# Keys projected in halves inside the recurrence of a two-block fp32 network

## The chip, the cores and the metric

One core of a Trainium2 chip runs the whole program in one launch. The metric is the time of one execution on the device in microseconds (us), lower is better; three runs of the kernel before gave 3436.60, 3443.00 and 3440.77.

## The reference

The input is 512 tokens of width 1024, all fp32. First come two mixing layers of three branches, with a feed-forward part behind each, then a second block that the change does not touch (a pooling layer and a dilated attention layer). A mixing layer, cut to what matters here:

```python
z = rms(x) @ w_in                            # conv q/k, v, o, gates, s_q, ckv, i_q, i_k, d_q, d_k, d_v, ...
h = mlstm(mq, mk, mv, i_pre, f_pre)          # recurrence over 4 chunks of 128 tokens, 4 heads of 128
y_a = sigmoid(m_o) * rms(h)
kv  = rms(s_ckv) @ w_kv_up                   # sparse keys and values
sq, sk = rope(rms(s_q)), rope(rms(kv[0]))    # 8 heads of 64; index scores choose 128 keys per token
y_b = sparse_attention(sq, sk, kv[1], rope(i_q), rope(i_k), i_w)
dq, dk = rope(rms(d_q)), rope(rms(d_k))      # 8 half heads of 64
y_c = rms(diff_attention(dq, dk, d_v, lam))
x = x + merged(gates, y_a, y_b, y_c) @ w_out
```

## The kernel before, in words

**Weights.** Every weight matrix comes as chunks of up to 128 x 1024 fp32. SP loads each into one of four slots RAW (`load`, line 316 on). POOL splits each into a high part WH and a low part WL with two slots each (`split`, L374, L375, L378), and may start on a chunk as soon as TensorE has finished the chunk two before it (`chunk_done`). TensorE multiplies high by high, high by low and low by high: `by_columns` (L405) with weights stationary, `by_tokens` (L454) with tokens stationary, two k tiles, four token tiles and 512 columns a chunk, so 24 matmuls.

**Order.** There is no planner. Each engine has a program written out by hand, and semaphores named after events tie them together; `claim(bank)` makes TensorE wait until the last reader of a PSUM bank has signalled. In a mixing layer TensorE does: convolution inputs, the small gates, ckvq, sq, mv, mo (lines 504 to 538); the sums of the gates (L542, L543, bank 5, copied by VectorE in L1554); transposes of the compressed keys and sparse queries (`to_features`, L492); kvup, two chunks that give sparse keys and values (L555, L558); the transposes of index queries and keys; then the recurrence.

**Recurrence** (lines 571 to 627 on TensorE, 1561 to 1639 on VectorE, 1159 to 1171 on ScalarE). For each of four chunks of tokens: a diagonal (L1565) is spread over the partitions by a ones matmul (L576), VectorE takes maxima and writes the arguments (L1569 to L1586), ScalarE takes exponentials, VectorE multiplies with q k (L581) in L1592 and weights the values (L1597); TensorE forms the state products (L596), turns the product (L604), forms the carried part (L613) and the values (L623); VectorE adds (L1606, L1614), updates the state (L1622 to L1627), divides and writes HALL (L1635 to L1638).

**After it.** TensorE projects the queries (dq), turns HALL and the sparse keys, projects the keys (dk), forms the index scores (L649), projects the values (dv) and turns queries and keys (lines 629 to 663). VectorE norms h, then runs `norm_and_turn` (line 1467: reductions of squares L1430, reciprocal L1423, tables L1451 to L1453, and for each of four tiles L1471, L1461, L1462, L1464, L1465) for the sparse keys, the queries and, after the index masks (lines 1657 to 1673), the keys. ScalarE, all of whose activations have line 1030, copies banks out, takes squares and roots. Then come the attentions, whose scores are L717 and which are interleaved with the gates (L679, L687).

Of the kernel before, what the change touches and what calls it, by code (L numbers as in the profile page):

```python
# [13 lines left out]
P = 128  # L14
T = 512
# [96 lines left out]
ROOTS = {"ckv": (256, 4), "sq": (S_DH, 32), "h": (M_DH, 16), "sk": (S_DH, 32), "dq": (S_DH, 32),  # L112
# [4 lines left out]
def build(nc, dram, weights, out):  # L117

    ctx = ExitStack()
    with ctx:  # L120
# [54 lines left out]
        SQUARED = {"ckv": TB[:, :, 0:256], "sq": TA, "h": HALL, "sk": TA, "dq": TB, "dk": TA}  # L175

        def square_of(name, m, width):
            where = YC[:, m, :] if name in ("ckv", "sq", "h") else MS[:, m * T:(m + 1) * T]
            return where[:, 0:width]
# [21 lines left out]
        RTOK = tiny(4)  # L201

# [183 lines left out]
        def _(pe):  # L386
# [53 lines left out]
            def by_tokens(outs, c, slot, ks, cols, hi, lo, n_k, shared=False):  # L440


                turns = [(w, n) for w in (WH, WL) for n in range(NT)]
# [52 lines left out]
            def layer(li):  # L496
# [37 lines left out]
                for name, banks, sem in (("ckvq", (5, 6, 7, 0), "ckvq_raw"), ("sq", (1, 2, 3, 4), "sq_raw"),  # L534
                                         ("mv", (5, 6, 7, 0), "v_ready"), ("mo", (1, 2, 3, 4), "mo_ready")):
# [23 lines left out]
                for n, b in enumerate((0, 1, 2, 3)):  # L559
# [6 lines left out]
                            lambda f: L("tr_copied", 9))  # L566


                pe.wait_ge(*L("mqk_ready", 8))
                pe.wait_ge(*L("v_ready", NT))  # L570
                for n in range(NT):
# [13 lines left out]
                    if n < NT - 1:  # L585
# [6 lines left out]
                        claim(2, 3)  # L592
# [8 lines left out]
                    claim(4)  # L601
                    pe.wait_ge(*L("sw_ready", n + 1))
                    for h in range(M_HEADS):
                        mm = nc.tensor.transpose(PS[4][:, h * P:(h + 1) * P], DM[:, h * P:(h + 1) * P],  # L604
                                                 IDENT[:, :])
                    mm.then_inc(L("swt_ready"), 1)
                    release[4] = L("swt_copied", n + 1)
# [1373 lines left out]
def lay_out(inputs):  # L1981
# [53 lines left out]
    def col(v):  # L2035
        return v.reshape(-1, P).T
# [57 lines left out]
```

## Time and profile before

| what | value |
| --- | --- |
| median of three runs | 3440.77 us |
| the profiled execution | 3439.93 us |
| its span, first to last instruction | 3438.3 us |
| mean granted TensorE clock | 0.954 |
| layer 0: projections end, recurrence starts, last totals, first scores | 168.85, 193.50, 259.10, 371.20 us |
| layer 1: the same | 1255.8, 1281.4, 1344.7, 1456.7 us |
| busy POOL | 1844.4 us, 54% |

The granted clock is 1.00 at 2.4 GHz and 0.50 at 1.2 GHz. Busy time of one instruction includes what it is held up in its engine. Matmuls follow each other faster than their durations say, since they overlap.

### The profile page before, as it was taken

What the parts mean: (1) busy time and instruction counts of PE and PEld (TensorE: products, weight loads), DVE (VectorE), ACT (ScalarE), POOL (GpSimd) and SP (SyncE); (2) the same over time, 40 slices, a digit from 0 to 9 for tenths busy, and PEclk for the clock granted to TensorE, in tenths of its full rate; (3) what the DMA queues carried; (4) which work ended last, traced back from release to release, by engine and by line L of the source; (5) the groups of instructions that cost most, each with busy time, mean ns of one, the idle gap of its engine ahead of it and who ended that gap; (6) DMA issues with size and microseconds to landing.
All of it is one profiled execution on the core that took longest, in us unless ns stands there. A gap on an engine that the chain in (4) does not pass through costs nothing.

```text
span 3438.3 us, 39007 instructions
## 1 busy us (share of the span) xinstructions
PE 3125.3 (91%) x14414; PEld 2575.1 (75%) x14414; DVE 1676.1 (49%) x2578; ACT 563.7 (16%) x1112; POOL 1844.4 (54%) x1621
## 2 busy tenths in 40 slices
PE   7957879999999986788999999989999999998998
PEld 5746657778878775666778887777778888887876
DVE  7647773464433665786265442455432222223543
ACT  2222223110000222223311000100011111121000
POOL 5603434566667651333366666675565555443665
PEclk9978989999999997898999999999999999999999
DMA  4201112233323320111133333332322222222322
GB/s 134 86 19 47 56 37 62 95 92 98 98 83 105 114 80 25 40 56 46 53 115 95 94 98 88 98 86 79 92 90 75 74 80 74 70 66 60 98 88 77
DMA packets 85371, 268.29 MB, mean 78 GB/s; under 512 B 9856, under 2 KB 10496, under 8 KB 85248
## 3 DMA queue, kind: packets, MB, share of 16 engines
q1 hardware_dynamic: 85248, 266.64, 25.7%
q8 instruction: 78, 1.28, 0.2%
q14 instruction: 45, 0.37, 0.0%
HBM read 262.41 MB, written 4.19 MB: 78 GB/s over the span
## 4 chain that ended last, share of the span: by engine, by line
PE 78%; DVE 17%; ACT 3%; issue 2%; DMA 0%; SPq 0%; DVEq 0%; POOL 0%; ACTq 0%
PE PS L405 52%; PE PS L454 11%; PE PS L687 3%; PE PS L679 3%; DVE MSK L1685 2%; DVE SMALLS L1684 2%; PE PS L915 1%; PE PS L740 1%; PE PS L941 1%; DVE MS L1730 1%; DVE TA L1471 1%; ACT MS L1030 1%; DVE TA L1465 1%; DVE SQ L1464 1%; PE PS L728 1%
## 5 line engine op out<-in xcount | busy, mean ns | idle before, releaser
L378 POOL TENSOR_TENSOR WL<-RAW,WH 128x1024 fp32r<-128x1024 f32 (+3 forms) x538 | 1208.2, 2246 | 44.8
L374 POOL TENSOR_TENSOR POOL_C<-POOL_C 128x1 f32<-128x1 f32 x538 | 124.2, 231 | 1525.7 <-PE PS L405 775.2
L405 PE MATMUL PS<-XNH,WH 128*128 128x512 f32 x1752 | 694.2, 396 | 14.8 <-DVE EYL L1401 9.1
L405 PE MATMUL PS<-XNL,WH 128*128 128x512 f32 x1752 | 686.5, 392 | 0.0
L375 POOL TENSOR_SCALAR WH<-RAW 128x1024 fp32r<-128x1024 f32 (+3 forms) x538 | 533.9, 992 | 0.3 <-issue 0.2
L405 PE MATMUL PS<-XNH,WL 128*128 128x512 f32 x1752 | 432.9, 389 | 0.0
L405 PEld LDWEIGHTS PS<-XNH,WH 128*128 128x128 f32 x1752 | 330.8, 189 | 88.3 <-DVE EYL L1401 10.3
L405 PEld LDWEIGHTS PS<-XNL,WH 128*128 128x128 f32 x1752 | 330.9, 189 | 69.1 <-issue 1.0
L405 PEld LDWEIGHTS PS<-XNH,WL 128*128 128x128 f32 x1752 | 328.2, 187 | 69.0
L454 PE MATMUL PS<-WH,XNH 128*128 128x512 f32 (+1 forms) x768 | 288.7, 376 | 0.0
L454 PE MATMUL PS<-WH,XNL 128*128 128x512 f32 (+1 forms) x768 | 286.9, 374 | 0.0
L1924 DVE SCALAR_TENSOR_TENSOR OQK<-PS,RT 128x512 f32<-128x512 f32 x48 | 33.1, 692 | 312.9 <-PE PS L405 307.0
L454 PE MATMUL PS<-WL,XNH 128*128 128x512 f32 (+1 forms) x768 | 176.0, 371 | 0.0
L454 PEld LDWEIGHTS PS<-WH,XNH 128*128 128x128 f32 x768 | 145.8, 190 | 22.6 <-issue 1.5
L454 PEld LDWEIGHTS PS<-WH,XNL 128*128 128x128 f32 x768 | 145.7, 190 | 20.3
L679 PE MATMUL PS<-XNH,WH 128*128 128x512 f32 x384 | 158.2, 412 | 0.0
L454 PEld LDWEIGHTS PS<-WL,XNH 128*128 128x128 f32 x768 | 140.9, 188 | 20.0
L679 PE MATMUL PS<-XNL,WH 128*128 128x512 f32 x384 | 152.4, 397 | 0.0
L405 PE MATMUL PS<-HH,WH 128*128 128x512 f32 x352 | 139.4, 396 | 7.3 <-DVE HL L1401 7.3
L405 PE MATMUL PS<-HL,WH 128*128 128x512 f32 x352 | 139.1, 395 | 0.0
L1799 DVE TENSOR_TENSOR HT<-SILU,PS 128x512 f32<-128x512 f32 x44 | 30.3, 688 | 202.1 <-PE PS L405 199.6
L1401 DVE TENSOR_TENSOR HL<-HT,HH 128x512 f32 (+1 forms) x44 | 112.6, 2559 | 5.1
(341 smaller groups left out, 4753.0 us busy)
## 6 DMA issues: line engine op xcount, KB each, us to landing
RAW<-w_oslot SPq DMA_DIRECT2D x56, 512.0 KB, 3.6
RAW<-w_L0ffn SPq DMA_DIRECT2D x44, 512.0 KB, 3.6
RAW<-w_L1ffn SPq DMA_DIRECT2D x44, 512.0 KB, 3.6
RAW<-w_od SPq DMA_DIRECT2D x32, 512.0 KB, 3.6
RAW<-w_epool SPq DMA_DIRECT2D x24, 512.0 KB, 3.6
RAW<-w_oslot SPq DMA_DIRECT2D x32, 384.0 KB, 3.0
RAW<-w_eug SPq DMA_DIRECT2D x16, 512.0 KB, 3.7
RAW<-w_eout SPq DMA_DIRECT2D x16, 512.0 KB, 3.6
```

The costliest lines, as they stand in the source:

```text
L374: nc.gpsimd.tensor_tensor(POOL_C[:, 1:2], POOL_C[:, 0:1], POOL_C[:, 0:1], ALU.add)
L375: nc.gpsimd.tensor_scalar(WH[:, half, 0:w], RAW[:, slot, 0:w], 1.0, 0.0, ALU.mult, ALU.add).then_inc(S("high_ready"), 1)
L378: nc.gpsimd.tensor_tensor(WL[:, half, 0:w], RAW[:, slot, 0:w], WH[:, half, 0:w].bitcast(F32), ALU.subtract).then_inc(S("weights_split"), 1)
L405: mm = nc.tensor.matmul(bank, w[:, slot, k * cols:(k + 1) * cols], x[:, k0 + k, :], start=first and j == 0 and w is WH and x is hi, stop=l ...
L454: mm = nc.tensor.matmul(outs[n], x[:, k, n * P:(n + 1) * P], w[:, slot, j * cols:(j + 1) * cols], start=k == 0 and w is WH and x is hi, st ...
L679: nc.tensor.matmul(PS[b][:, :], WH[:, c % 2, k * P:(k + 1) * P], x[:, k, :], start=k == 0 and x is XNH, stop=False)
L687: mm = nc.tensor.matmul(PS[b][:, :], WL[:, c % 2, k * P:(k + 1) * P], XNH[:, k, :], start=False, stop=k == KD - 1)
L728: mm = nc.tensor.transpose(PS[4][:, m * P:(m + 1) * P], SS[:, q % 2, src, m * P:(m + 1) * P], IDENT[:, :])
L740: mm = nc.tensor.matmul(PS[7][:, h * d:(h + 1) * d], TB[:, j, m * P:(m + 1) * P], V[:, m, h * d:(h + 1) * d], start=m == 0, stop=m == n)
L1401: V.tensor_tensor(dst_lo, src, dst_hi.bitcast(F32), ALU.subtract).then_inc(sem, 1)
L1684: then(V.max(TOP8, m))
L1685: then(V.match_replace(m, TOP8, m, TAKEN))
```

## The change

The query projection dq is placed behind mo, in banks 5, 6, 7, 0, and its raw values go to YA (as DQR). The key projection becomes two segments, dkA and dkB, of four chunks each with the same weights: each chunk is loaded and split twice, and TensorE multiplies it with token tiles 0 and 1 in the first segment and 2 and 3 in the second, 12 matmuls a time, one chunk behind the key transposes and one behind the values of each chunk of the recurrence (`half_of_keys`), in banks 4 and 5. The raw keys go to TB (as DKR). VectorE takes the roots of queries and sparse keys ahead of the recurrence and keeps them (RSQ, RSK, both new), keeps two sets of tables, and norms and turns one of eight tiles at each of eight places in the recurrence (`fill`). Inside the recurrence the state products move behind the carried part, the last chunk's are skipped as before, and the banks are dealt out anew. Behind it come the transposes of queries, dv, HALL, the index scores, sparse keys and keys; VectorE norms the keys ahead of the low halves and the masks. Four chunks a layer are added.

The diff, cut. What is left out: `by_tokens` gets a parameter `tiles`; the order of ROOTS, the buffers of squares (HALL for dq and sk) and the arguments `keep` and `t`; `norm_tile` is the body of the loop of `norm_and_turn`; the weights of dkA and dkB on the host.

```diff
--- before
+++ after
@@ -55,8 +55,8 @@
-    ("mv", 4, [1024]), ("mo", 4, [1024]), ("kvup", 2, [1024]),
-    ("dq", 4, [1024]), ("dk", 4, [1024]), ("dv", 4, [1024]),
+    ("mv", 4, [1024]), ("mo", 4, [1024]), ("dq", 4, [1024]), ("kvup", 2, [1024]),
+    ("dkA", 4, [1024]), ("dkB", 4, [1024]), ("dv", 4, [1024]),
     ("gA", 8, [1024, 512]), ("gC", 8, [1024, 512]), ("gB", 8, [1024, 512]), ("wout", 8, [1024]),
...
@@ -532,7 +534,8 @@
-                                         ("mv", (5, 6, 7, 0), "v_ready"), ("mo", (1, 2, 3, 4), "mo_ready")):
+                                         ("mv", (5, 6, 7, 0), "v_ready"), ("mo", (1, 2, 3, 4), "mo_ready"),
+                                         ("dq", (5, 6, 7, 0), "dq_raw")):
...
@@ -564,7 +567,21 @@
+                pe.wait_ge(*L("tr_copied", 9))
+                def half_of_keys(step):
+                    name, q = ("dkA", "dkB")[step // 4], step % 4
+                    tiles = (0, 1) if name == "dkA" else (2, 3)
+                    if q == 0:
+                        claim(4, 5)
+                    c = seg(name) + q
+                    by_tokens({n: PS[4 + n % 2][:, :] for n in tiles}, c, c % 2, (2 * q, 2 * q + 1), T,
+                              XNH, XNL, KD, tiles=tiles)
+                    if q == 3:
+                        for n in tiles:
+                            release[4 + n % 2] = L("dk_raw", n + 1)
...
@@ -589,6 +606,25 @@
+                    half_of_keys(2 * n)
+                    claim(b)
+                    pe.wait_ge(*L("sw_ready", n + 1))
+                    for h in range(M_HEADS):
+                        mm = nc.tensor.transpose(PS[b][:, h * P:(h + 1) * P], DM[:, h * P:(h + 1) * P],
+                                                 IDENT[:, :])
...
+                        for h in range(M_HEADS):
+                            mm = nc.tensor.matmul(
+                                PS[(1, 7 - n % 2)[h // 2]][:, h % 2 * 129:h % 2 * 129 + 129],
+                                MQK[:, h, tok], CT[:, h * 129:(h + 1) * 129], start=True, stop=True)
+                        mm.then_inc(L("n2_ready"), 1)
+                        release[1] = release[7 - n % 2] = L("n2_taken", n)
+                    if n < NT - 1:
                         claim(2, 3)
                         pe.wait_ge(*L("ktm_copied", n + 1))
                         pe.wait_ge(*L("vw_ready", n + 1))
...
@@ -598,66 +634,41 @@
                     mm.then_inc(L("n1_ready"), 1)
-                    release[banks[0]] = release[banks[1]] = L("tot_ready", n + 1)
-                token_group(f"L{li}dq", (1, 2, 3, 4))
-                for n, b in enumerate((1, 2, 3, 4)):
-                    release[b] = L("dq_raw", n + 1)
+                    release[1] = release[0] = L("tot_ready", n + 1)
+                    half_of_keys(2 * n + 1)
+                pe.wait_ge(*L("dq_normed", 1))
+                to_features(lambda n, f: DQR[:, n, f * P:(f + 1) * P], 4, (6, 7, 2, 3), L("tr_ready"),
+                            lambda f: L("tr_copied", f + 10))
+                token_group(f"L{li}dv", (0, 1, 4, 5))
+                for n, b in enumerate((0, 1, 4, 5)):
+                    release[b] = L("dv_ready", n + 1)
                 pe.wait_ge(*L("ya_tm", NT))
-                to_features(lambda n, f: HALL[:, n, f * P:(f + 1) * P], 4, (0, 5, 6, 7), L("tr_ready"),
+                to_features(lambda n, f: HALL[:, n, f * P:(f + 1) * P], 4, (6, 7, 2, 3), L("tr_ready"),
                             lambda f: L("ya_low", f + 1))
-                pe.wait_ge(*L("sk_normed", 1))
-                to_features(lambda n, f: TA[:, n, f * P:(f + 1) * P], 4, (5, 6, 7, 0), L("tr_ready"),
-                            lambda f: L("tr_copied", f + 14))
-                token_group(f"L{li}dk", (1, 2, 3, 4))
-                for n, b in enumerate((1, 2, 3, 4)):
-                    release[b] = L("dk_raw", n + 1)
-                pe.wait_ge(*L("tr_copied", 9))
                 for n in range(1, NT):
...
                     for h in range(IDX_HEADS):
-                        b = (5, 6, 7, 0)[h]
+                        b = (0, 1, 4, 5)[h]
...
-                token_group(f"L{li}dv", (1, 2, 3, 4))
-                for n, b in enumerate((1, 2, 3, 4)):
-                    release[b] = L("dv_ready", n + 1)
-                pe.wait_ge(*L("dq_normed", 1))
-                to_features(lambda n, f: TB[:, n, f * P:(f + 1) * P], 4, (5, 6, 7, 0), L("tr_ready"),
+                pe.wait_ge(*L("sk_normed", 1))
+                to_features(lambda n, f: TA[:, n, f * P:(f + 1) * P], 4, (6, 7, 2, 3), L("tr_ready"),
                             lambda f: L("tr_copied", f + 18))
                 pe.wait_ge(*L("dk_normed", 1))
...
@@ -1141,50 +1152,57 @@
+                chunk(seg("dq") + 4)
+                for n, b in enumerate((5, 6, 7, 0)):
+                    run(DQR[:, n, :], PS[b][:, :], ACT.Copy, L("dq_raw"), scale=RTOK[:, n:n + 1])
                 for f in range(2):
                     take(6 + f, CKVH[:, f, :], T, f + 1)
                 for f in range(4):
                     take(f, SQT[:, f, :], T, f + 3)
+                root("dq")
                 if li:
                     act.wait_ge(S("x_saved"), 16 * KD)
                 chunk(seg("kvup") + 1)
                 for n, b in enumerate((4, 5, 6, 7)):
                     run(TA[:, n, :], PS[b][:, :], ACT.Copy, L("sk_raw"))
+                square("sk")
                 chunk(seg("kvup") + 2)
                 for n, b in enumerate((0, 1, 2, 3)):
                     run(SV[:, n, :], PS[b][:, :], ACT.Copy, L("sv_ready"))
                 for f in range(2):
                     take(4 + f, IQT[:, f, :], T, f + 7)
                 take(6, IKT[:, :], T, 9)
+                root("sk", squares=False)
...
+                    if n == 2:
+                        chunk(seg("dkA") + 4)
+                        for m in range(2):
+                            run(DKR[:, m, :], PS[4 + m][:, :], ACT.Copy, L("dk_raw"), scale=RTOK[:, m:m + 1])
                     act.wait_ge(*L("darg_ready", n + 1))
...
                         act.wait_ge(*L("n1_ready", n))
-                    run(SWT, PS[4][:, :], ACT.Copy, L("swt_copied"))
+                    run(SWT, PS[6 + n % 2][:, :], ACT.Copy, L("swt_copied"))
+                chunk(seg("dkB") + 4)
+                for m in range(2, 4):
+                    run(DKR[:, m, :], PS[2 + m][:, :], ACT.Copy, L("dk_raw"), scale=RTOK[:, m:m + 1])
                 root("h")
-                chunk(seg("dq") + 4)
-                for n, b in enumerate((1, 2, 3, 4)):
-                    run(TB[:, n, :], PS[b][:, :], ACT.Copy, L("dq_raw"), scale=RTOK[:, n:n + 1])
-                root("sk")
                 for f in range(4):
-                    take((0, 5, 6, 7)[f], YAH[:, f, :], T, f + 10, scale=col(li, "m_norm_g")[:, f:f + 1])
-                square("dq")
+                    take((6, 7, 2, 3)[f], DQT[:, f, :], T, f + 10)
+                root("dk")
+                chunk(seg("dv") + 4)
+                for n, b in enumerate((0, 1, 4, 5)):
+                    run(DV[:, n, :], PS[b][:, :], ACT.Copy, L("dv_ready"), scale=RTOK[:, n:n + 1])
                 for f in range(4):
-                    take((5, 6, 7, 0)[f], SKT[:, f, :], T, f + 14)
-                root("dq", squares=False)
-                chunk(seg("dk") + 4)
-                for n, b in enumerate((1, 2, 3, 4)):
-                    run(TA[:, n, :], PS[b][:, :], ACT.Copy, L("dk_raw"), scale=RTOK[:, n:n + 1])
-                square("dk")
-                act.wait_ge(*L("dq_normed", 1))
...
@@ -1550,6 +1570,8 @@
+                squares(S_HEADS, "dq", keep=RSQ)
+                dq_tables = rope_tables(row("dq_g"), 1)
...
@@ -1557,6 +1579,17 @@
+                dve.wait_ge(*L("tr_ready", 9))
+                sk_tables = rope_tables(row("sk_g"))
+                squares(S_HEADS, "sk", keep=RSK)
+                def fill(step):
+                    if step < 4:
+                        norm_tile(DQR, step, RSQ, dq_tables, "dq")
+                    else:
+                        norm_tile(TA, step - 4, RSK, sk_tables, "sk")
...
@@ -1587,6 +1620,7 @@
+                    fill(2 * n)
...
@@ -1607,8 +1641,9 @@
+                    fill(2 * n + 1)
                     dve.wait_ge(*L("n1_ready", n + 1))
-                    for e, b in enumerate((5, 0)):
...
@@ -1646,12 +1681,8 @@
-                dve.wait_ge(*L("sk_raw", NT))
-                dve.wait_ge(*L("tr_ready", 9))
-                norm_and_turn(TA, "sk_g", "sk")
-                low_halves((0, 5, 6, 7), YAH, YAL, 10, "ya_low", gain=lambda f: col(li, "m_norm_g")[:, f:f + 1])
-                dve.wait_ge(*L("dq_raw", NT))
-                norm_and_turn(TB, "dq_g", "dq")
+                norm_and_turn(DKR, "dk_g", "dk")
+                low_halves((6, 7, 2, 3), YAH, YAL, 14, "ya_low", gain=lambda f: col(li, "m_norm_g")[:, f:f + 1])
...
@@ -1671,8 +1702,6 @@
-                dve.wait_ge(*L("dk_raw", NT))
-                norm_and_turn(TA, "dk_g", "dk")
```

## Rows read from the trace of the kernel before

**Rows 1.** The page's part 1: busy time, share and instructions of each engine.
```profile
...
PE 3125.3 (91%) x14414; PEld 2575.1 (75%) x14414; DVE 1676.1 (49%) x2578; ACT 563.7 (16%) x1112; POOL 1844.4 (54%) x1621
```

**Rows 2.** Stages: stretch, length, busy PE, PEld, DVE, ACT, POOL; PEclk, DMA share, GB/s.
```profile
...
168.85:177.15 8.30, 3.20 (x29) 2.96 (x28) 7.91 (x27) 5.35 (x10) 3.62 (x3) 0.97 0.41 125
177.15:189.70 12.55, 12.54 (x50) 10.26 (x51) 0.71 (x2) 2.07 (x4) 3.59 (x3) 0.88 0.07 7
189.70:193.50 3.80, 1.31 (x12) 1.08 (x11) 0.00 (x0) 3.54 (x7) 3.55 (x3) 1.00 0.28 114
193.50:259.10 65.60, 36.65 (x150) 30.50 (x151) 32.88 (x96) 9.97 (x19) 0.00 (x0) 0.66 0.03 8
259.10:371.20 112.10, 84.09 (x378) 68.72 (x376) 88.57 (x122) 31.82 (x59) 47.54 (x36) 0.85 0.17 50
1255.80:1264.10 8.30, 3.22 (x29) 2.96 (x29) 7.92 (x26) 5.35 (x10) 3.60 (x3) 0.88 0.37 123
1264.10:1277.60 13.50, 13.48 (x50) 10.89 (x51) 0.72 (x2) 2.07 (x5) 3.59 (x3) 0.82 0.06 11
...
1281.40:1344.70 63.30, 34.84 (x149) 29.05 (x150) 32.87 (x96) 9.97 (x19) 0.00 (x0) 0.68 0.03 9
```

**Rows 3.** The chain that ended last, layer 0: start, us, engine and line.
```profile
...
259.00 21.80 PE PS L454 x96
```

**Rows 4.** PE's timeline, layer 0: start, us, line, tiles, idle time and its releaser.
```profile
...
177.16 0.77 PE L454 MATMUL PS<-WH,CKVH 128*128 128x512 f32 x1 [5.11 <-DVE SMALLS L1554]
```

**Rows 5.** Stretches on DVE: stretch, length, busy (operations), PEclk, DMA share, GB/s.
```profile
...
135.20:158.20 23.00, 22.58 (x21) 1.00 0.33 92
288.00:299.40 11.40, 10.99 (x21) 0.50 0.00 0
...
264.20:275.90 11.70, 11.43 (x9) 1.00 0.20 52
332.30:341.20 8.90, 7.71 (x15) 0.73 0.09 28
```

**Rows 6.** Timeline around 138 us, POOL and DVE.
```profile
...
138.29 2.71 POOL L378 TENSOR_TENSOR WL<-RAW,WH 128x1024 fp32r<-128x1024 f32 x1
...
138.78 2.77 DVE L1471 TENSOR_TENSOR TA<-TA,SMALLS 128x512 f32<-128x512 f32 x1
```

**Rows 7.** Timeline of one chunk (n = 1) of the recurrence, layer 0.
```profile
...
210.94 2.05 PE L576 MATMUL PS<-MS,ONES 128*128 128x512 f32 x2 [3.42 <-DVE MS L1565]
...
215.98 0.69 DVE L1586 TENSOR_TENSOR MS<-MS,SMALLS 128x512 f32<-128x512 f32 x1
...
217.47 0.69 DVE L1592 TENSOR_TENSOR MS<-MS,PS 128x512 f32<-128x512 f32 x1 [0.80 <-ACT SMALLS L1030]
...
218.91 2.06 PE L596 MATMUL PS<-MS 128*128 128x129 f32 x8 [3.94 <-DVE MS L1597]
...
221.62 1.93 PE L613 MATMUL PS<-MS,MQK 128*128 128x129 f32 x8
...
223.34 1.61 PE L623 MATMUL PS<-VEXT,MS 128*128 128x129 f32 x8
...
225.05 0.76 DVE L1614 TENSOR_TENSOR MS<-MS,PS 128x258 f32<-128x258 f32 x2 [0.71 <-PE PS L623]
...
229.78 2.05 PE L576 MATMUL PS<-MS,ONES 128*128 128x512 f32 x2 [4.83 <-DVE MS L1565]
```

**Rows 8.** Groups of ACT, 259.1 to 300 us: count, busy us, mean ns, idle before.
```profile
...
L1030 ACT ACTIVATE MS<-TA 128x512 f32<-128x512 f32 x4 | 2.2, 642 | 0.0
...
L1030 ACT ACT_TABLE_LOAD x1 | 1.3, 1283 | 0.0
```

**Rows 9.** Groups of DVE, 281 to 288 us.
```profile
...
L1430 DVE TENSOR_REDUCE SMALLS<-MS 128x8 f32<-128x512 f32 x4 | 2.5, 678 | 8.1 <-ACT MS L1030 8.1
...
L1451 DVE TENSOR_TENSOR TMP<-COS,ROW 128x256 f32<-128x256 f32 x1 | 0.4, 426 | 0.0
L1423 DVE RECIPROCAL SMALLS<-SMALLS 128x32 f32<-128x32 f32 x1 | 0.4, 354 | 0.4 <-ACT SMALLS L1030 0.4
```

More of the change, by code:

```diff
@@ L173, in build @@
         SS = MS[:, :].rearrange("p (b j w) -> p b j w", b=2, j=4)
-        SQUARED = {"ckv": TB[:, :, 0:256], "sq": TA, "h": HALL, "sk": TA, "dq": TB, "dk": TA}
+        DQR, DKR = YA, TB
+        SQUARED = {"ckv": TB[:, :, 0:256], "sq": TA, "h": HALL, "sk": TA, "dq": DQR, "dk": DKR}
         def square_of(name, m, width):
-            where = YC[:, m, :] if name in ("ckv", "sq", "h") else MS[:, m * T:(m + 1) * T]
-            return where[:, 0:width]
+            where = {"ckv": YC, "sq": YC, "dq": HALL, "sk": HALL, "h": YC}.get(name)
+            return MS[:, m * T:m * T + width] if where is None else where[:, m, 0:width]
         at = [0]
@@ L438, in first_pair, with by_tokens @@
                     mm.then_inc(S("chunk_done"), 1)
-            def by_tokens(outs, c, slot, ks, cols, hi, lo, n_k, shared=False):
-                turns = [(w, n) for w in (WH, WL) for n in range(NT)]
+            def by_tokens(outs, c, slot, ks, cols, hi, lo, n_k, shared=False, tiles=range(NT)):
+                turns = [(w, n) for w in (WH, WL) for n in tiles]
                 if shared:
@@ L1194, in layer @@
                         w = (n + 1) * P
-                        run(RELU[:, i % 2, 0:w], PS[(5, 6, 7, 0)[h]][:, 0:w], ACT.Relu, L("relu_ready"))
-                root("dk", squares=False)
-                chunk(seg("dv") + 4)
-                for n, b in enumerate((1, 2, 3, 4)):
-                    run(DV[:, n, :], PS[b][:, :], ACT.Copy, L("dv_ready"), scale=RTOK[:, n:n + 1])
+                        run(RELU[:, i % 2, 0:w], PS[(0, 1, 4, 5)[h]][:, 0:w], ACT.Relu, L("relu_ready"))
                 for f in range(4):
-                    take((5, 6, 7, 0)[f], DQT[:, f, :], T, f + 18)
+                    take((6, 7, 2, 3)[f], SKT[:, f, :], T, f + 18)
                 for f in range(4):
-                    take((1, 2, 3, 4)[f], DKT[:, f, :], T, f + 22)
+                    take((0, 1, 4, 5)[f], DKT[:, f, :], T, f + 22)
                 for a in range(2):
@@ L1417, in over, with ask_root, squares @@
                     return ap.unsqueeze(1).to_broadcast([P, h, ap.shape[-1]])
-                def ask_root(name):
+                def ask_root(name, keep=None):
                     _, n = ROOTS[name]
                     dve.wait_ge(*L("root_taken", ROOT_NO[name]))
-                    then(V.reciprocal(RSH[:, 0:n], RSH[:, 0:n]))
-                def squares(h, name):
+                    then(V.reciprocal((RSH if keep is None else keep)[:, 0:n], RSH[:, 0:n]))
+                def squares(h, name, keep=None):
                     for n in range(NT):
@@ L1465, in turn, with norm_tile @@
                     return V.tensor_tensor(dst, straight, turned, ALU.add)
+                def norm_tile(buf, n, roots_, tables, name):
+                    then(V.tensor_tensor(heads(buf[:, n, :], 8), heads(buf[:, n, :], 8),
+                                         bcast(roots_[:, 8 * n:8 * n + 8], 8, S_DH), ALU.mult))
+                    ins = turn(buf[:, n, :], 8, tables[0][:, n, :], tables[1][:, n, :],
+                               heads(buf[:, n, :], 8))
+                    if n < NT - 1:
+                        then(ins)
+                    else:
+                        ins.then_inc(L(f"{name}_normed"), 1)
+                        dve.wait_ge(*L(f"{name}_normed", 1))
                 def norm_and_turn(buf, gain, name):
                     squares(S_HEADS, name)
[L1469 removed]
+                    tables = rope_tables(row(gain))
                     for n in range(NT):
[L1471 to L1477 removed]
+                        norm_tile(buf, n, RSH, tables, name)
                 then(V.memset(CONVIN[:, :, 0:3], 0.0))
```

54 lines of the change are left out of this document (20 added, 34 removed).

## The prediction

> **What bounds the kernel now.** The page comes first: TensorE is busy for 91% of the span [rows 1], so a gain has to come from time in which it waits or runs at its lower clock. The table of stages says where that is [rows 2]. I call P the end of the last projection (168.85 us in layer 0), S the start of the recurrent part (193.50), R the moment at which VectorE adds the last chunk's totals (259.10), and Q the first attention scores (371.20). From P to Q 202.3 us pass; layer 1 has the same legs, 25.6 us to S and 63.3 to R. In the recurrence TensorE is busy 36.6 of 65.6 us at a mean granted clock of 0.66, VectorE 32.9 us, POOL never. After it, TensorE is busy 84.1 of 112.1 us, VectorE 88.6.
>
> The chain of waits gives the reason for the tail: the query projection runs bare for 21.8 us [rows 3], then VectorE norms the sparse keys with TensorE idle, and the last thing before Q is VectorE's norm of the keys. Ahead of the recurrence TensorE stands 5.1 us until VectorE has copied the gate sums out of bank 5 (line 1554) [rows 4]. So this stretch is a relay: TensorE streams while VectorE has little, then VectorE turns tiles while TensorE has nothing. Two prices matter most [rows 5]: four tiles normed and turned take 11.4 us with POOL silent and 23.0 us with POOL splitting weights, 2.85 against 5.7 us a tile. Why shows in [rows 6]: a multiply of VectorE with both inputs in SBUF, 0.69 us elsewhere [rows 7], starts just after POOL's subtraction and ends only behind it, 2.77 us long.
>
> The Trainium skill ("SBUF — State Buffer", the section "Who interferes with whom") has the rule: a GpSimd operation and a VectorE one with two SBUF inputs exclude each other for a whole instruction. The trace agrees (0.69 against 2.77 us). It speaks against this change.
>
> **The change, part by part.** I add in three legs, each against the same leg of before.
>
> *Leg 1, P to S.* The query projection moves here: four chunks, 21.8 us [rows 3]. It covers the tile work of VectorE that ran past P, which should end TensorE's 5.1 us wait. But what is late next is the same bank 5: VectorE copies the gate sums only after the squares of the queries and their tables. I follow ScalarE from P+21.8: four copies of queries, two and four transposed tiles, ten activations in 5.35 us [rows 2], P+27.2; four squares, 2.2, P+29.4; one more table load, 1.3 [rows 8], P+30.7. The reductions run beside the squares; root and reciprocal 0.8, three table products 1.1, the copy 0.2 [rows 9], so kvup starts at P+33 instead of P+8.3. Its 48 matmuls take 12.55 us as before (13.5 in layer 1), since the idle time ahead of them (about 7 us) again lets the clock fall. From the end of kvup to S it was 3.8 us. Now VectorE must wait for the index-key transposes (1.3), make the sparse keys' tables while POOL splits the next chunk (until 3.6 us after kvup [rows 2]), reduce four squares (2.5 [rows 9]), take the reciprocal behind the root (0.8) and form the diagonal (0.7): 7.7. So P to S is 33 + 13 + 7.8 = 53.8 us against 24.7 and 25.6: **+28.7**, that is 21.8 for the projection and 7 of new waiting.
>
> The Trainium skill ("ScalarE: Activation LUTs", the section "What ACT_TABLE_LOAD costs") puts another 1.38 us of drain behind each load; by the page leg 1 would be 1.4 longer. No row shows it: the load of [rows 8] is 1.28 us and nothing follows it.
>
> *Leg 2, S to R.* I walk one middle chunk, PE's spread of the diagonal at 0 [rows 7]. The arguments are ready at 5.75, as before. Then a tile, 2.85, takes the place of the 0.80 us wait for the exponential: 8.6. Product 0.7: 9.3. TensorE has meanwhile run its half of a key chunk, 12 matmuls, from 4.0 to 6.7 at the higher clock or 9.4 at the lower (half of the 5.4 us of a whole chunk, or twice that half), so it is mostly hidden. Turning the product 0.9, carried part 1.7, VectorE's read 0.8: 12.7. The second tile: 15.5. TensorE needs until 15.6 for the state products (2.0, now behind the carried part) and the values (1.5). From the totals to the next spread it was 4.7: 20.3, against 18.8 before. The second half chunk lies beside those 4.7 us.
>
> On top comes POOL: eight chunks instead of none are split here, 3.6 us each [rows 2], and each starts when a half chunk ends. Its bounds: nothing, if it falls on reductions, on operations reading PSUM or on VectorE's waits, and 2.9 us where SBUF work wants to run (the 11.6 us between the two prices of [rows 5], over four splits). Laid beside the walk, the first split of a chunk delays the weighting of the values a little, the second the division, HALL and the diagonal by some 2 us. I take 1.7 a period: 22. The first chunk has no carried part but its first split falls on a tile: 20.8; the last ends at its totals, 15.5. Sum 20.8 + 22 + 22 + 15.5 = 80.3 against 65.6 and 63.3: **+15.8**. Bounds: 70 with no blocking and the higher clock, 103 with full blocking and the lower one.
>
> The four extra chunks a layer cost 512 KB each on a queue that is nearly idle here (DMA share 0.03 [rows 2]); SP issues them as slots come free and nothing else is queued there. Nothing, unless POOL's ring falls behind the halves; at one split in 10 us it does not.
>
> *Leg 3, R to Q.* The query chunks (21.8) and key chunks leave it, and so do two norms. VectorE now sets it. HALL is ready at about R+3. The key copies stand ahead of the squares of h on ScalarE, then squares, load, root: multiplies from R+6.5. They take 8.6, between 5.5 (eight by 0.69) clean and 11.7 with POOL at two splits [rows 5], as one split meets them here: R+15. Reductions, root, reciprocal and tables 4.4: R+19.5. Four tiles 11.4, plus 2.9 for each of two splits of dv: R+36.7. Low halves four by 0.7: R+39.4. Masks 8.9 [rows 5]: R+48.3. ScalarE's last two index copies done, it moves eight tiles at 0.54 [rows 2], then scores: R+53. dv itself (21.8) ends near R+27 and is hidden. Against 112.1: **-59.1**. Bounds: 48 and 60.
>
> Per layer 28.7 + 15.8 - 59.1 = -14.6, for two layers -29.2 us. The profiled execution is 3439.93, 0.8 below the median of 3440.77, so I set the sum against the median: **3411.6**. Moved banks, YA and TB as buffers, and the kept roots change no duration; POOL's 28 us more of splits have no other cover to lose.
>
> **The rivals.**
> (1) *POOL and VectorE lock each other through the recurrence: slower.* Place: leg 2. Each of eight splits costs its full 2.9 to 3.6 us instead of the 0.6 that I count on average, +19, and at the lower clock the half chunks (5.4 us each) push the spread of the diagonal back, +4. Leg 2 is then 103 us, the layer +8: 3457. It decides from a period of 26.5 us on, where the 14.6 are used up. For it: [rows 5] and [rows 6]. Against: at least 5 us of VectorE's period read PSUM or reduce, 4 are waits. The rule from the skill named above gives this result. Chance 0.12.
> (2) *The denser stream keeps the clock high.* Filled periods have TensorE busy some 16 of 20 us where it was 10 of 18.8, and the clock fell in those gaps. Spread, carried part and values would lose half their time, about 2 us a period, kvup 1.6: 10 a layer more: 3392. Against: VectorE is nearly closed up, so shorter matmuls only shorten its waits. Chance 0.20.
> (3) *The new waits are larger than walked.* The bank 5 wait and the root chain of h behind the key copies each cost 4 us more: 3428. Chance 0.22.
> (4) *Nothing to measure:* 3441. The freed tail is just given back by legs 1 and 2, leg 2 at 95 us. Chance 0.10.
> Forecast itself 0.36.
>
> **How the numbers follow.** About 0.2%, 7 us, is what a measurement can tell from no change. Forecast, (2) and most of (3) are faster by more: 0.73. (4) and a bit of (3): 0.13. (1) and the edge of (4): 0.14. The range runs from just under (2) to short of (4): 3388 to 3438; it leaves out (1) and most of (4), which hold 0.2.
>
> **What would show it.** Right: TensorE still stands about 7 us ahead of kvup, with the copy of the gate sums as releaser; S at P+54; periods of 21 to 23 us in the recurrence; POOL busy some 29 us there; dk_normed near R+37; scores at R+53; P to Q near 188 us in both layers. Wrong: kvup starting at P+27, periods above 26.5 or under 19, or a tail over 60 us.

## The result, and the profile after

Four runs of the changed kernel gave 3414.81 to 3420.44 us, median 3416.36, against 3439.92 for the kernel before beside it: a ratio of 0.9934 (0.9916 to 0.9951). The forecast was 3411.6. The profiled execution is 3414.81 us, its span 3412.6, 25.7 less than before.

The page's parts 1 and 2 of the kernel after:

```profile
span 3412.6 us, 39047 instructions
...
PE 3113.2 (91%) x14414; PEld 2558.3 (75%) x14414; DVE 1681.3 (49%) x2578; ACT 564.2 (17%) x1114; POOL 1867.9 (55%) x1645
...
PEclk9988889999999997888999999999999999999999
```

TensorE runs as many matmuls as in [rows 1] and is busy 12 us less; POOL has the 24 instructions of eight more splits, three each. Between S and R it runs 21 instructions, so seven splits: the first two of the eight key chunks are split ahead of S, and the first chunk of values is split ahead of R. The table of stages of the kernel after, first three stages for leg 1 (P is 167.13, the first stretch starts 0.17 us behind it), then legs 2 and 3, then legs 2 and 3 of layer 1; columns as in [rows 2]:

```profile
167.30:199.84 32.54, 25.48 (x126) 20.81 (x124) 14.63 (x34) 11.44 (x20) 18.05 (x15) 0.98 0.33 95
199.84:213.47 13.63, 13.63 (x50) 11.01 (x51) 0.00 (x1) 4.26 (x8) 3.59 (x3) 0.80 0.06 9
213.47:221.98 8.51, 1.31 (x13) 1.10 (x11) 6.49 (x9) 3.86 (x8) 3.81 (x3) 0.81 0.36 112
221.98:305.95 83.97, 54.01 (x235) 43.17 (x236) 66.21 (x137) 9.57 (x18) 27.69 (x21) 0.76 0.16 44
305.95:357.25 51.30, 41.18 (x196) 32.10 (x194) 42.43 (x66) 24.04 (x46) 18.87 (x15) 0.85 0.12 37
1290.90:1377.40 86.50, 54.17 (x235) 43.44 (x236) 68.20 (x137) 9.58 (x18) 27.37 (x21) 0.76 0.15 43
1377.40:1428.80 51.40, 41.37 (x195) 32.23 (x193) 42.42 (x66) 24.00 (x46) 18.88 (x15) 0.85 0.13 36
```

The legs, layer 0 / layer 1, in us (an ordinary table, worked out from such rows of each kernel):

| leg | before | after | change | forecast |
| --- | --- | --- | --- | --- |
| 1, P to S | 24.7 / 25.6 | 54.8 / 54.4 | +30.1 / +28.8 | +28.7 |
| 2, S to R | 65.6 / 63.4 | 84.0 / 86.5 | +18.4 / +23.1 | +15.8 |
| 3, R to Q | 112.1 / 111.8 | 51.3 / 51.5 | -60.8 / -60.3 | -59.1 |
| P to Q | 202.3 / 200.8 | 190.1 / 192.3 | -12.2 / -8.5 | -14.6 |

Legs 1 and 3 are within 1.7 us of the working. Leg 2 is 2.6 and 7.3 us over. The two layers together gain 20.7 us where 29.2 were forecast; the span is 25.7 shorter, so 5 us more come from code that the change does not touch. Nearly all of it lies between Q of layer 0 and P of layer 1: 884.7 us before, 879.3 after, and 878.6 to 887.5 in the ten kernels below, which have the same code there. I can't tell these 5 us from such variation.

What stands ahead of the first product of kvup, PE's timeline of the kernel after (columns as in [rows 4]):

```profile
199.84 0.77 PE L456 MATMUL PS<-WH,CKVH 128*128 128x512 f32 x1 [6.22 <-DVE SMALLS L1576]
```

Line 1576 is the copy of the gate sums (L1554 in [rows 4]). The wait of 5.11 us did not end: it is 6.22 long, at P+32.7. The walk said about 7, and P+33.

Chunk n = 1 of the recurrence, timeline of PE, DVE and POOL of the kernel after, against [rows 7]:

```profile
241.47 1.10 PE L593 MATMUL PS<-MS,ONES 128*128 128x512 f32 x2
...
241.69 1.04 POOL L377 TENSOR_SCALAR WH<-RAW 128x1024 fp32r<-128x1024 f32 x1
...
242.60 0.69 DVE L1602 TENSOR_REDUCE SMALLS<-PS 128x4 f32<-128x512 f32 x1 [1.28 <-PE PS L593]
242.81 2.38 POOL L380 TENSOR_TENSOR WL<-RAW,WH 128x1024 fp32r<-128x1024 f32 x1
...
247.27 1.04 POOL L377 TENSOR_SCALAR WH<-RAW 128x1024 fp32r<-128x1024 f32 x1
247.29 1.29 DVE L1475 TENSOR_TENSOR SQ<-YA,TMP 128x256 f32<-128x256 f32 x1
248.39 2.38 POOL L380 TENSOR_TENSOR WL<-RAW,WH 128x1024 fp32r<-128x1024 f32 x1
248.50 2.55 DVE L1476 TENSOR_TENSOR SQ<-YA,TMP 128x256 f32<-128x256 f32 x1
...
253.25 1.09 PE L613 MATMUL PS<-IDENT,MS 128*128 128x128 f32 x4 [6.63 <-DVE MS L1626]
254.13 1.93 PE L622 MATMUL PS<-MS,MQK 128*128 128x129 f32 x8
...
262.27 2.66 POOL L380 TENSOR_TENSOR WL<-RAW,WH 128x1024 fp32r<-128x1024 f32 x1
262.65 2.29 DVE L1670 SCALAR_TENSOR_TENSOR SMALLS<-MS 128x4 f32<-128x4 f32 x1
...
266.83 2.04 PE L593 MATMUL PS<-MS,ONES 128*128 128x512 f32 x2 [5.99 <-DVE MS L1598]
```

From spread to spread 25.36 us pass, and three splits fall into them. The first meets reductions and a read of PSUM, which take 0.69 us each as elsewhere; only an operation of four columns behind them is held, by 0.4 us. At the second the multiplication with the cosines (L1475) starts 0.02 us behind POOL's rounding and takes 1.29 us instead of 0.43; the next starts 0.11 us behind POOL's subtraction and takes 2.55 instead of 0.42; and an operation on four numbers a partition (L1670) starts 0.38 us behind the third split's subtraction and takes 2.29. TensorE has run its half chunk meanwhile and stands 6.63 us, then 5.99, and comes back at the lower clock (the second spread takes 2.04 us at a granted clock of 0.50, where the first took 1.10).

### The profile page after: what moved, and what is told of

Same layout as the page of the kernel before. It is cut to its first block, busy times and chain, and to the rows that moved or that the text cites. A ratio compares the mean times of both kernels' runs of the same rounds, so it can differ in the third digit from the quotient of the medians.

```text
span 3412.6 us, 39047 instructions
## 1 busy us (share of the span) xinstructions
PE 3113.2 (91%) x14414; PEld 2558.3 (75%) x14414; DVE 1681.3 (49%) x2578; ACT 564.2 (17%) x1114; POOL 1867.9 (55%) x1645
## 4 chain that ended last, share of the span: by engine, by line
PE 80%; DVE 16%; ACT 3%; issue 1%; DMA 0%; SPq 0%; DVEq 0%; POOL 0%; ACTq 0%
PE PS L407 52%; PE PS L456 13%; PE PS L698 3%; PE PS L690 3%; DVE MSK L1714 2%; DVE SMALLS L1713 2%; PE PS L926 1%; PE PS L751 1%; PE PS L952 1%; DVE MS L1759 1%; PE PS L739 1%; DVE MS L1513 1%; ACT MS L1041 1%; PE PS L940 1%; PE PS L420 1%
## 5 line engine op out<-in xcount | busy, mean ns | idle before, releaser
L380 POOL TENSOR_TENSOR WL<-RAW,WH 128x1024 fp32r<-128x1024 f32 (+3 forms) x546 | 1225.0, 2244 | 45.5
L377 POOL TENSOR_SCALAR WH<-RAW 128x1024 fp32r<-128x1024 f32 (+3 forms) x546 | 539.9, 989 | 0.5 <-issue 0.5
L456 PEld LDWEIGHTS PS<-WH,XNH 128*128 128x128 f32 x768 | 147.5, 192 | 25.4 <-ACT TB L1041 4.2
L456 PEld LDWEIGHTS PS<-WH,XNL 128*128 128x128 f32 x768 | 147.1, 192 | 20.3
L456 PEld LDWEIGHTS PS<-WL,XNH 128*128 128x128 f32 x768 | 142.0, 189 | 20.5
```

Of the source, the lines that this page charges most:

```text
L377: nc.gpsimd.tensor_scalar(WH[:, half, 0:w], RAW[:, slot, 0:w], 1.0, 0.0, ALU.mult, ALU.add).then_inc(S("high_ready"), 1)
L380: nc.gpsimd.tensor_tensor(WL[:, half, 0:w], RAW[:, slot, 0:w], WH[:, half, 0:w].bitcast(F32), ALU.subtract).then_inc(S("weights_split"), 1)
L456: mm = nc.tensor.matmul(outs[n], x[:, k, n * P:(n + 1) * P], w[:, slot, j * cols:(j + 1) * cols], start=k == 0 and w is WH and x is hi, st ...
```

## The experiments

All of them start from the changed kernel. The theory was: leg 1 is set by bank 5 and then by the roots and tables of the sparse keys; leg 2 is VectorE's chain plus what POOL's splits hold it up; leg 3 is VectorE's chain again. Single runs have no interval; they are read by their legs. The kernel before, run beside them, gave 3441.2, 3439.1 and 3432.9 us on the three chips.

### Bank 5 earlier

```diff
-                squares(S_HEADS, "dq", keep=RSQ)
-                dq_tables = rope_tables(row("dq_g"), 1)
                 dve.wait_ge(*L("bg_ready", 1))
                 V.tensor_copy(BG, PS[5][:, 0:32]).then_inc(L("bg_taken"), 1)
                 dve.wait_ge(*L("bg_taken", 1))
+                squares(S_HEADS, "dq", keep=RSQ)
+                dq_tables = rope_tables(row("dq_g"), 1)
```

> VectorE copies the gate sums out of bank 5 before the squares of the queries and their tables, nothing else. Theory (bank 5 is what kvup waits for, as forecast in leg 1): kvup starts right behind the low halves of the compressed keys, at P+26 to P+27 instead of P+32.5, the recurrence starts 5 to 6 us sooner in each layer, and the kernel takes 10 to 12 us less than the changed one, about 3405. Rival (the root chain of the sparse keys is late anyway): kvup starts sooner but the recurrence does not, and the time stays within 3 us.

Measured: 3395.49 us (3389.27 to 3400.42), 0.9872 of before (0.9856 to 0.9889); P to S 46.2 in both layers, 8.7 and 8.2 less. Table of stages, P to kvup, kvup, kvup to S:

```profile
168.19:194.70 26.51, 25.64 (x125) 20.95 (x124) 10.87 (x24) 6.96 (x13) 18.05 (x15) 1.00 0.31 97
194.70:205.87 11.17, 11.17 (x50) 9.20 (x51) 3.81 (x10) 8.75 (x16) 3.59 (x3) 1.00 0.25 57
205.87:214.37 8.50, 1.31 (x12) 1.09 (x11) 6.49 (x9) 3.85 (x8) 3.81 (x3) 0.75 0.34 113
```

The wait is gone: kvup starts at P+26.5, 6.2 earlier. The other 2.5 us of layer 0 are the clock. With no stand ahead of it kvup runs at 1.00 and takes 11.17 us, against 13.63 at 0.80 after TensorE had stood 6.22 us. The theory held, but 5 to 6 us a layer was short: it left out what the clock gives back. Leg 2 came out 2.1 and 1.4 us shorter as well, which nothing here explains. This is the one cheap mistake in the change, a copy of 0.19 us queued behind the squares of the queries and their tables, which it doesn't need; putting it right nearly doubles the gain.

### Splits of eight columns in the recurrence

```diff
+                if isinstance(c, int) and any(FIRST[f"L{li}dkA"] <= c < FIRST[f"L{li}dv"] + 2 for li in range(DEPTH)):
+                    w = 8
```

> POOL writes only 8 of 1024 columns in the splits of the key chunks and of the first two value chunks, so key and value projections are computed on leftover weights; everything else is as in the changed kernel. Theory (VectorE and POOL exclude each other): the recurrence falls from 84 to 72 to 75 us a layer, no operation of VectorE in it is over 0.8 us, the kernel takes about 20 us less. Rival (the half chunks in TensorE's order and its clock hold the recurrence up): the operations of VectorE get shorter but the recurrence stays over 80 us, and the kernel takes under 8 us less.

Measured: 3377.45 us, one run, 39 less than the kernel after; leg 2 68.5 and 68.8 us, 15.5 and 17.7 less; leg 1 1.7 and 2.1 less; leg 3 the same within 0.5. Table of stages, S to R:

```profile
222.77:291.30 68.53, 50.41 (x235) 40.47 (x236) 54.43 (x137) 9.58 (x18) 6.08 (x21) 0.85 0.18 54
```

With the same 137 operations, VectorE is busy 54.43 us instead of 66.21. So the splits hold it 11.8 us, seven of them, 1.7 each (13.8 us in layer 1). Added up by operation in the kernel after, each of the seven holds it 0.4 to 3.0 us. TensorE never waits for POOL in this leg, in either kernel, so the splits cost nothing by being late. The other 3.7 of the 15.5 us are its idle time: 17.8 us of it with full splits (83.97 less 66.21), 14.1 with thin ones. At least part of that is the clock, 0.76 against 0.85: TensorE's answers come later. The same operations of VectorE in groups by form, S to R, in the kernel after (first fence) and with thin splits (second); columns: count, busy us, mean ns, idle before:

```profile
L1483 DVE TENSOR_TENSOR TA<-TA,SMALLS 128x512 f32<-128x512 f32 x4 | 4.2, 1058 | 0.1
L1476 DVE TENSOR_TENSOR SQ<-YA,TMP 128x256 f32<-128x256 f32 x4 | 3.8, 953 | 0.0
L1631 DVE TENSOR_TENSOR MS<-VEXT,SMALLS 128x516 f32<-128x516 f32 x3 | 3.5, 1166 | 0.0
L1662 DVE TENSOR_TENSOR MS<-MS 128x516 f32<-128x516 f32 x2 | 3.0, 1482 | 0.1
...
L1626 DVE TENSOR_TENSOR MS<-MS,PS 128x512 f32<-128x512 f32 x4 | 2.7, 686 | 0.1
...
L1670 DVE SCALAR_TENSOR_TENSOR SMALLS<-MS 128x4 f32<-128x4 f32 x3 | 2.6, 868 | 0.0
```

```profile
L1485 DVE TENSOR_TENSOR TA<-TA,SMALLS 128x512 f32<-128x512 f32 x4 | 2.8, 688 | 0.1
L1628 DVE TENSOR_TENSOR MS<-MS,PS 128x512 f32<-128x512 f32 x4 | 2.8, 688 | 0.1
L1633 DVE TENSOR_TENSOR MS<-VEXT,SMALLS 128x516 f32<-128x516 f32 x3 | 2.1, 689 | 0.0
L1478 DVE TENSOR_TENSOR SQ<-YA,TMP 128x256 f32<-128x256 f32 x4 | 1.7, 418 | 0.0
L1664 DVE TENSOR_TENSOR MS<-MS 128x516 f32<-128x516 f32 x2 | 1.4, 696 | 0.1
L1672 DVE SCALAR_TENSOR_TENSOR SMALLS<-MS 128x4 f32<-128x4 f32 x3 | 0.5, 157 | 0.0
```

(Lines stand two higher in the second kernel.) The multiply that reads PSUM, L1626, costs the same in both; those with two inputs in SBUF are the ones that grow. The middle periods without the blocking are 18.3 and 18.6 us (18.3 and 19.3 in layer 1), so the walk's 20.3 was too long and its 1.7 for POOL far too short.

### The tiles behind the recurrence

```diff
-                    fill(2 * n)
...
-                    fill(2 * n + 1)
...
+                for step in range(8):
+                    fill(step)
                 squares(4, "h")
```

> All eight tiles of queries and sparse keys are normed and turned behind the recurrence, the key halves stay in it. Theory (VectorE sets both the recurrence and the tail): the recurrence takes 68 to 73 us, the tail grows from 51 to about 80, P to Q is about 205 against 190: the kernel takes 25 to 35 us more than the changed one, near 3447. Rival (TensorE's halves set the period): the recurrence stays at 80 us or more and the kernel is over 3460.

Measured: 3427.76 us, one run; leg 2 64.9 and 65.8, leg 3 72.8 in both, P to Q 193.0 in both. Both legs are shorter than expected, leg 2 by 3 us at least and leg 3 by 7, and the whole is 19 us faster than the theory had it. Eight tiles cost 19.0 and 20.6 us inside the recurrence and 21.5 and 21.4 behind it; between P and Q 190.1 and 192.3 stand against 193.0. With the halves inside, where the tiles stand therefore decides 1 to 3 us a layer. Of the 11.4 us that this run takes over the kernel after, 8.2 lie between Q of layer 0 and P of layer 1, in code that is the same.

### The half chunks behind the recurrence

```diff
-                    half_of_keys(2 * n)
...
-                    half_of_keys(2 * n + 1)
...
+                for step in range(8):
+                    half_of_keys(step)
```

> The eight half chunks of keys run behind the recurrence, the tiles stay in it, ScalarE's copies of the raw keys all come behind it. Theory: the recurrence has no splits beside it and takes 74 to 77 us, the tail grows by the 21.8 us of keys that ScalarE waits for ahead of the norm of h, to about 72; P to Q is near 201: 20 to 25 us more than the changed kernel, about 3438. Rival (halves hidden or not is the same, since VectorE is the bound everywhere): within 5 us of the changed kernel.

Measured: 3441.10 us, one run: the whole gain is gone. Table of stages, S to R:

```profile
224.20:298.10 73.90, 37.91 (x151) 31.86 (x152) 54.39 (x136) 8.42 (x16) 0.00 (x0) 0.66 0.00 1
```

P to Q is 204.8 and 203.9 us, leg 2 73.9 and 74.1, leg 3 75.7 and 75.3, all within 4 us of the theory. VectorE is busy 54.39 us here and 54.43 with thin splits, with no blocking in either, yet the leg is 73.9 against 68.5. What differs is that TensorE has little to do and its clock is 0.66 instead of 0.85. That is rival 2 measured apart from the blocking: the denser stream is worth 5.4 us in this leg (5.3 in layer 1). In the kernel after POOL's blocking eats it and more. The middle periods are 20.3 and 20.5 us here, the walk's clean period.

### Both behind

The two edits above together.

> The changed kernel with both the eight tiles and the eight half chunks behind the recurrence: of the change only the move of the query projection and the kept roots are left. Theory (tiles and halves are each other's cover, and VectorE's tiles bring nothing in the recurrence but need the halves as cover behind it): P to S 54.7, S to R 62 to 65 as in the kernel before, R to Q 76 to 80, together near 196, that is 4 to 6 us a layer over the changed kernel, about 3427. Rival (interleaving in the recurrence is what the change gains): P to Q over 202, at or above the kernel before, 3440.

Measured: 3463.04 us, one run, 1.0088 of before; legs of layer 0 55.3, 63.6 and 95.9, P to Q 214.8 (layer 1: 213.3). The theory fell (it had P to Q near 196), the rival held. A stretch of the tail in the table of stages, then its timeline:

```profile
312.00:335.00 23.00, 20.36 (x95) 15.86 (x94) 22.69 (x16) 4.62 (x7) 20.15 (x15) 1.00 0.35 105
```

```profile
302.73 2.70 POOL L380 TENSOR_TENSOR WL<-RAW,WH 128x1024 fp32r<-128x1024 f32 x1
303.22 2.77 DVE L1483 TENSOR_TENSOR YA<-YA,SMALLS 128x512 f32<-128x512 f32 x1
...
307.10 0.50 PE L456 MATMUL PS<-WH,XNH 128*128 128x512 f32 x1 [0.41 <-POOL WH L377]
307.13 2.43 POOL L380 TENSOR_TENSOR WL<-RAW,WH 128x1024 fp32r<-128x1024 f32 x1
307.24 2.60 DVE L1476 TENSOR_TENSOR SQ<-YA,TMP 128x256 f32<-128x256 f32 x1
```

A half chunk is 12 matmuls, 3.0 us at the full clock, but needs a whole split of 3.6 us or more. One behind the other they make POOL and VectorE hold each other (busy 20.15 and 22.69 of 23 us), and TensorE waits for POOL at each half, for the high part and again for the low one. Each of VectorE's tiles of queries meets two splits: about 8.7 us a tile, against 2.85 clean. So halves are cheap only where a split has time to hide, which is inside the recurrence. The price of moving them out is 13 us a layer with the tiles inside (204.8 and 203.9 against 190.1 and 192.3) and 21 with the tiles out. The tiles in turn are worth 10.0 and 9.4 us inside when the halves are out, where they were worth 2.9 and 0.7 with the halves in.

### The sparse keys' tables earlier

On top of the earlier bank 5, the tables are made ahead of the wait for the index keys, in a buffer of their own (X, saved by then):

```diff
-                dve.wait_ge(*L("tr_ready", 9))
-                sk_tables = rope_tables(row("sk_g"))
+                if li:
+                    dve.wait_ge(S("x_saved"), 16 * KD)
+                sk_tables = rope_tables(row("sk_g"), X[:, 7, :])
                 squares(S_HEADS, "sk", keep=RSK)
...
+                dve.wait_ge(*L("tr_ready", 9))
                 norm_and_turn(DKR, "dk_g", "dk")
```

> As bank5_early, and the tables of the sparse keys go to a free tile of X, so that VectorE makes them and takes the roots during kvup and does not wait for the index-key transposes. Theory (that wait and the tables behind POOL's split are what follows kvup): kvup's end to the recurrence falls from 8.5 to about 5 us, P to S from 46 to about 43, some 3388. Rival (ScalarE's copies decide): no change of P to S.

Measured: 3388.20 us, one run; P to S 42.7 in both layers, 3.5 less than with bank 5 alone, as the theory had it. From the end of kvup to S 5.0 us are left of 8.5.

### The key copies earlier on ScalarE

```diff
+                    if n == 2:
+                        chunk(seg("dkA") + 4)
...
                     if n < NT - 1:
...
-                    if n == 2:
-                        chunk(seg("dkA") + 4)
...
+                square("h")
                 chunk(seg("dkB") + 4)
...
-                root("h")
+                root("h", squares=False)
```

The copies of dkA go ahead of the copy of the turned keys of chunk 2 (KTM), the squares of h ahead of the copies of dkB.

> The changed kernel with ScalarE's order alone altered: the first two key copies come before the copy of the turned keys of chunk 2, and the squares of h before the last two key copies. Theory: TensorE no longer waits 1.9 us for bank 4 in the third period (23.2 to about 21.5) and VectorE's norm of h starts about 2 us sooner (tail 51.4 to about 49): 4 us a layer, about 3408. Rival (VectorE is closed up, so a wait of TensorE or ScalarE costs nothing): under 1 us a layer.

Measured: 3423.47 us, one run, where the theory had 3408; P to Q 192.4 and 191.2. The tail is 50.0 and 49.9, 1.3 and 1.5 less; leg 2 is 87.4 and 86.8, 3.4 and 0.4 more. The wait for bank 4 is gone, but VectorE is held up longer in the same leg (70.16 us busy against 66.21 in layer 0). A wait taken away in a stretch that two engines contend for can just move the next meeting.

### All three together

> bank5_early, sk_tables_early and copies_early in one. Theory (the three waits lie one behind another): P to S about 43, S to R about 81, R to Q about 49, near 173 together, about 3380. Rival (one hides another): no better than bank5_early at 3395.

Measured: 3386.89 us (3383.82 to 3389.74), 0.9844 of before (0.9828 to 0.9861). Table of stages, the three legs of layer 0:

```profile
168.97:211.70 42.73, 38.14 (x186) 31.31 (x184) 22.11 (x43) 19.45 (x36) 25.26 (x21) 0.99 0.29 87
211.70:292.60 80.90, 54.76 (x241) 43.10 (x242) 67.78 (x137) 11.25 (x21) 27.36 (x21) 0.82 0.17 51
292.60:342.70 50.10, 39.20 (x191) 30.46 (x189) 43.77 (x66) 22.51 (x43) 18.84 (x15) 0.90 0.13 38
```

This is the lowest time of a kernel that computes everything: 52 us under before, twice the change's own gain. It can't be told from the single run of the kernel without the earlier key copies (3388.20): P to Q is 173.7 and 177.7 us here and 176.2 and 175.2 there, the same sum.

### Tiles ahead of the recurrence

On top of all three: three tiles of queries behind the gates' copy, with the first place of the last three chunks empty (`tiles_ahead`, the diff), or one tile ahead, with the first place of the last chunk alone empty (`one_ahead`):

```diff
+                for tile in range(3):
+                    norm_tile(DQR, tile, RSQ, dq_tables, "dq")
                 sk_tables = rope_tables(row("sk_g"), X[:, 7, :])
...
-                    fill(2 * n)
+                    if n == 0:
+                        fill(3)
...
-                    fill(2 * n + 1)
+                    fill(4 + n)
```

> As all_early, but three of the eight tiles are normed and turned before the recurrence, beside kvup, where VectorE is idle for some 14 us; the fourth query tile stays in the first chunk and one sparse key tile in each chunk, behind the carried part. Theory (VectorE's work and POOL's lock set the recurrence): S to R falls by 9 to 13 us, P to S grows by 4 to 6, so about 6 us a layer less than all_early, near 3368. Rival (the tiles only filled waits in the recurrence and were free there): S to R falls by under 4 us and the kernel is slower than all_early.

> As all_early, with one query tile ahead of the recurrence beside kvup and seven in it. Theory: the tile ahead costs 6 us of VectorE because it meets one split of kvup, and the sparse keys' roots are then just in time: P to S 43 to 45; the recurrence loses one tile and at most one collision, 3 to 5 us: 1 to 3 us a layer less than all_early, near 3383. Rival (as with tiles_ahead, what is saved inside is paid ahead): within 2 us of all_early.

Measured: three tiles ahead, 3389.56 us, 0.9854 (0.9838 to 0.9870); one tile ahead, 3391.33 us, 0.9868 (0.9851 to 0.9886). Both theories fell and their rivals held. With three, leg 2 falls by 7 and 9 us to 73.9 and 76.0, and leg 1 grows by 9.2 in both layers, where 4 to 6 were expected. The place beside kvup looked free, but POOL splits there too, timeline with three tiles ahead:

```profile
202.81 2.72 POOL L380 TENSOR_TENSOR WL<-RAW,WH 128x1024 fp32r<-128x1024 f32 x1
203.30 2.51 DVE L1477 TENSOR_TENSOR SQ<-YA,TMP 128x256 f32<-128x256 f32 x1
```

With one tile ahead leg 1 grows by 3.6 and leg 2 shrinks by 1.5 and 3. Leg 3 is 2.3 to 2.6 us longer in both kernels; with one tile ahead 1.9 us of that come from a split that meets the last division and HALL in layer 0 (0.92 and 2.71 us instead of 0.16 and 1.59). The tiles' time is paid ahead, and nothing is won.

## Why the prediction was right

The forecast of a faster kernel, 3411.6 us, stands 4.8 us from the measured median, by legs that hold one by one except the second. The number is nearer than the working: between P and Q the two layers gained 20.7 us of the 29.2, and the 5 us from code that the change doesn't touch, which the sum had at nothing, brought the total back. That is luck.

**Leg 1 held, for the reason given.** kvup at P+32.7 for P+33, the gate-sum copy as releaser, S at P+54.8 and 54.4 for 53.8. Moving that copy alone took 8.4 us off, and the second wait, roots and tables, was confirmed by taking out 3.5 of it. The walk had what the edit by itself hides: TensorE is given 21.8 us of cover, and the wait merely moves behind it, since the same engine copies the bank last.

**Leg 2 is the step that was mis-sized, in two terms that partly cancel.** The walk said "20.3" for a clean period; thin splits measure 18.3. It said "I take 1.7 a period" for POOL, some 5 us over the leg. Thin splits take 15.5 and 17.7 us off the leg, over 2 us for each of its seven splits (the walk counted eight), inside the bounds of 0 and 2.9 but nearer the upper one. (11.8 of the 15.5 are VectorE held up; the rest is what follows, TensorE's answers later and at a lower clock.) For layer 0 the walk without POOL is some 7 us too long (75.5 for 68.5), its term for POOL some 10 too short, and the two leave 3.7. The clean period was long because the walk took the spread and the carried part at the lower clock: 2.05 and 1.93 us in [rows 7], 1.10 and 1.07 with thin splits. With the halves behind the recurrence, where no split runs and the clock is 0.66, the periods are 20.3 and 20.5, as walked. PE's timeline with thin splits:

```profile
239.71 1.10 PE L595 MATMUL PS<-MS,ONES 128*128 128x512 f32 x2 [0.72 <-DVE MS L1600]
...
248.56 1.07 PE L624 MATMUL PS<-MS,MQK 128*128 128x129 f32 x8
...
258.03 1.10 PE L595 MATMUL PS<-MS,ONES 128*128 128x512 f32 x2 [2.26 <-DVE MS L1600]
```

POOL's term was short because of where the walk laid the splits: the first of a chunk was to cost "a little", the second "some 2 us". They start when a half chunk ends. One of the seven, the one at 241.5 us, fell on reductions and reads of PSUM and cost 0.4; the others met a tile or the state update, nearly all SBUF work, and chunk n = 1 took three splits that held VectorE 5.8 us in all. Even L1670, on four columns, waited 2.1 us. The rule of the Trainium skill ("SBUF — State Buffer", the section "Who interferes with whom") that was set against this change holds in the rows of this leg, and so does its exception: L1626 reads PSUM and takes 0.69 us at 231.33 us, inside a subtraction that runs from 230.84 to 233.50. So the middle periods were 23.2 to 25.4 us, over the 21 to 23 that the text named as the sign, and short of the 26.5 at which rival 1 would have decided.

**Leg 3 held:** 51.3 and 51.5 us for 53, with the keys normed at R+36.9 for R+36.7. The last figure is closer than its parts: the norm of h began at R+8.5 for R+6.5, and the four tiles took 16.0 us for 17.2. It was set by VectorE's chain as walked; moving ScalarE's copies took 1.3 and 1.5 off.

**The rivals.** Rival 1 (the lock) is the right mechanism at some 60% of its price: it wanted 23 us on top of the 5 counted, and 15.5 and 17.7 were there. It decides where splits come one behind the other, in the tail of the kernel with both behind. Rival 2 (the clock) is real and worth 5.4 us in leg 2 and 2.4 in kvup, but the lock covered it in the one and a stand of 6.2 us spoiled it in the other. Rival 3 wanted 4 us more at bank 5 and 4 behind the key copies; kvup started 0.3 us ahead of the walk, and leg 3 ended 1.7 and 1.5 ahead of it. Rival 4 (nothing to measure) wanted leg 2 at 95 us; it took 84.0 and 86.5, and the interval of the ratio ends at 0.9951.

**Where the gain of the change comes from.** With neither tiles nor halves in the recurrence, P to Q takes 214.8 and 213.3 us, 12.5 more in each layer than in the kernel before. Tiles and halves together bring 24.7 and 21.0 back, and they are not independent. The tiles look like the change's point, but with the halves in they bring only 2.9 and 0.7 us; with the halves out they bring 10.0 and 9.4. The halves bring 13 us a layer with the tiles in and 21 with them out. So the gain stands or falls with the half chunks, which fill TensorE's waits at a pace at which their splits are partly hidden.

Left open: the 5 us between the layers; how the 12.5 us divide between the moved query projection and the doubled splits, since no kernel here has the one without the other; and how much would be left if each split fell where VectorE reduces or reads PSUM. No kernel here tried that; the one split that fell there by itself cost 0.4 us.

## What to carry to other kernels

When work is moved under another stretch, ask what the filler brings along on the engines that look idle: here each half chunk needed a whole split on GpSimd, and that cost VectorE 11.8 us, more than the tiles' own move gained. Price such a meeting by what stands at the moment it starts, not by an average over the period, and measure it by shrinking one side's operations to a few columns. Then look for the small read that frees a bank: a copy of 0.19 us, put ahead of the reductions it had queued behind, was worth 17 us ahead of the two recurrences.

## What the runs showed of the hardware that was not expected

The lock works in both directions: in the kernel after, some of POOL's roundings (L377) take 1.49 to 1.56 us instead of 1.05 where VectorE came first (at 297.18 us, 0.11 us behind a multiplication of VectorE). And a tiny operation can pay as much as a large one: one of 128x4 took 2.29 us where it takes 0.16.

A stand of TensorE costs more than itself: kvup took 13.63 us at a granted clock of 0.80 behind 6.22 us of idle time, and 11.17 us at 1.00 without.

A table load on ScalarE had nothing ahead of it or behind it. Timeline of ACT of the kernel after, the root of the queries:

```profile
194.26 2.26 ACT L1041 ACTIVATE HALL<-YA 128x512 f32<-128x512 f32 x4
196.54 1.28 ACT L1041 ACT_TABLE_LOAD   x1
197.83 0.32 ACT L1041 ACTIVATE SMALLS<-SMALLS,EPS_C 128x32 f32<-128x32 f32 x1
```

The load starts 0.02 us after the squares end, the root 0.01 us after the load. The 1.38 us of drain that the Trainium skill ("ScalarE: Activation LUTs", the section "What ACT_TABLE_LOAD costs") adds to each load do not show here, and the sum was right to go by the row.
